# NSA scores: the keys' low parts on 64 rows, with the tiles' query parts in alternate row halves and two tiles beside each other

## What is computed

```
s_s = einsum('bqghd,bgqkld->bghqkl', qb, k_sel) * scale   # selected blocks
s_w = einsum('bqghd,bsgd->bghqs', qb, kw) * scale         # window of 512
o   = gate0 * o_c + gate1 * o_s + gate2 * o_w             # o_s, o_w: softmax(scores - slope*distance) @ values
```

## Time and profile before

| | us |
|---|---|
| median of three executions | 2296.42 |
| the profiled execution, span from its first to its last instruction | 2294.8 |
| the profiled execution's own time | not recorded apart from the span |
| input projection of the NSA mixer, from about | 745 to 832 |
| NSA mix: first scores to last turn, about | 832 to 976 |

### The profile page before, as it was taken

The page is one execution under the profiler, slowest core; times in us unless marked ns, Lnnn a source line. Parts: engine busy times, 40 slices in busy tenths (PEclk is TensorE's granted clock), DMA queues, the critical chain, the costliest instruction groups (busy, mean ns, idle before and its releaser), DMA issues.

```text
span 2294.8 us, 34769 instructions
## 1 busy us (share of the span) xinstructions
PE 2247.6 (98%) x14151; PEld 1950.4 (85%) x14151; DVE 1641.8 (72%) x2121; ACT 1051.0 (46%) x1515; POOL 634.8 (28%) x559
## 2 busy tenths in 40 slices
PE   7999999999999999999999999999999999999999
PEld 5888778999887877778999888999887868899987
DVE  6668557889785456637888657989456984788844
ACT  4322534555334457734555346444345363544432
POOL 0110223332122048803332011332011870233200
PEclk9999999999999999999999999999999999999999
DMA  8654156775763210026774526775333202787322
GB/s 333 191 166 140 46 174 165 185 180 122 267 211 102 82 57 1 1 65 168 190 185 119 162 95 173 175 185 120 101 97 98 81 30 76 191 191 173 105 92 83
DMA packets 224373, 308.69 MB, mean 135 GB/s; under 512 B 14345, under 2 KB 165446, under 8 KB 223958
## 3 DMA queue, kind: packets, MB, share of 16 engines
q1 hardware_dynamic: 173268, 223.99, 30.1%
q0 software_dynamic: 50640, 82.29, 17.4%
q10 hardware_dynamic: 306, 0.19, 0.0%
HBM read 302.23 MB, written 4.19 MB: 134 GB/s over the span
## 4 chain that ended last, share of the span: by engine, by line
PE 85%; DVE 9%; POOL 2%; ACT 2%; issue 1%; DMA 1%; ACTq 0%; DVEq 0%
PE ps L733 42%; PE ps L1181 10%; PE ps L1183 10%; PE ps L1182 10%; PE ps L880 4%; DVE w_lo L2320 2%; DVE dsa_mask L3127 1%; PE ps L1307 1%; POOL nsa_p L3498 1%; PE ps L1323 1%; DVE small L3125 1%; PE ps L929 1%; ACT w_hi L1635 1%; DMA m_raw<-in_ada_w 1%; DVE h_lo L2417 1%
## 5 line engine op out<-in xcount | busy, mean ns | idle before, releaser
L2320 DVE TENSOR_TENSOR w_lo<-w_raw,w_hi 128x1024 fp32r<-128x1024 f32 (+1 forms) x466 | 652.5, 1401 | 478.7 <-ACT w_hi L1635 477.0
L1635 ACT ACTIVATE w_hi<-w_raw 128x1024 fp32r<-128x1024 f32 (+1 forms) x472 | 495.7, 1051 | 996.0 <-PE ps L733 577.6
L1181 PE MATMUL ps<-feat_t,w_hi 128*128 128x256 f32 x1152 | 326.5, 283 | 3.1 <-DVE hid L2824 2.3
L1182 PE MATMUL ps<-feat_t,w_hi 128*128 128x256 f32 x1152 | 326.0, 283 | 0.0
L1183 PE MATMUL ps<-feat_t,w_lo 128*128 128x256 f32 x1152 | 326.0, 283 | 0.0
L3351 POOL TENSOR_TENSOR w_raw<-w_raw,w_raw 128x1024 f32<-128x1024 f32 x72 | 177.7, 2468 | 456.8 <-DVE w_lo L2320 456.8
L733 PE MATMUL ps<-h_hi,w_hi 128*128 128x512 f32 (+1 forms) x712 | 279.7, 393 | 3.8 <-DVE w_lo L2320 2.2
L733 PE MATMUL ps<-h_lo,w_hi 128*128 128x512 f32 (+1 forms) x712 | 277.2, 389 | 0.0
L733 PE MATMUL ps<-h_hi,w_lo 128*128 128x512 f32 (+1 forms) x712 | 277.2, 389 | 0.0
L1181 PE MATMUL ps<-h_hi,w_hi 128*128 128x256 f32 x864 | 244.9, 283 | 1.9 <-DVE w_lo L2320 1.9
L1182 PE MATMUL ps<-h_lo,w_hi 128*128 128x256 f32 x864 | 244.5, 283 | 0.0
(11 more groups left out here) (464 smaller groups left out, 4219.2 us busy)
## 6 DMA issues: line engine op xcount, KB each, us to landing
w_raw<-in_ffn_w_up SPq DMA_DIRECT2D x126, 512.0 KB, 6.5
w_raw<-in_ffn_w_down SPq DMA_DIRECT2D x176, 256.0 KB, 3.3
w_raw<-in_ffn_w_up POOLq DMA_DIRECT2D x72, 512.0 KB, 7.6
m_raw<-in_ada_w POOLq DMA_DIRECT2D x56, 512.0 KB, 4.7
w_raw<-in_ffn_w_gate SPq DMA_DIRECT2D x54, 512.0 KB, 5.9
w_raw<-in_hg_w_in SPq DMA_DIRECT2D x64, 256.0 KB, 3.1
w_raw<-in_ffn_w_up SPq DMA_DIRECT2D x48, 256.0 KB, 3.1
w_raw<-in_nsa_w_in SPq DMA_DIRECT2D x40, 256.0 KB, 2.9
```

What stands on the lines that cost most here:

```text
L1181: K.nc.tensor.matmul(out, hi[:, w], m_hi, start=opens and kt == f == 0, stop=False, skip_group_check=True)
L1182: K.nc.tensor.matmul(out, hi[:, w], m_lo, start=False, stop=False, skip_group_check=True)
L1635: K.nc.scalar.activation(K.half(K.hi(u), width), K.half(K.raw(u), width), ACT.Copy) \
L2320: K.nc.vector.tensor_tensor(K.half(K.lo(u), width), K.half(K.raw(u), width), hi, ALU.subtract) \
```

## The change

The keys' low part is multiplied with the queries' high part alone, on 64 rows; low times low is left out. For tiles 0 and 2 the high part now lies in the other row half and the low part in the head's own half, for tiles 1 and 3 as before. So the two low products of a pair of tiles lie in different row halves. The pairs are (3, 2) and (0, 1); in each, both products over 128 rows come first and then both over 64 rows. In the projection each head's high part and low part are written by two instructions of 64 x 256 instead of one of 64 x 512.

```diff
+def high_rows(head, t):
+    return own_rows(head + (t in (0, 2)))
+
+def token_groups(t):
+    by_tile = t.rearrange("p (a s b) -> p a s b", s=2, b=P)
+    return by_tile[:, :, 0, :], by_tile[:, :, 1, :]
...
-            nc.tensor.matmul(out, K.nq[:, head, tok], K.nk[:, i + 4 * br, 0:w], start=True, stop=False)
-            nc.tensor.matmul(out, K.nq[:, head, tok], K.nk_lo[:, i + 4 * br, 0:w], start=False, stop=True) \
+        def key_high(t):
+            if u:
+                pe.wait_ge(*K["nsa_max"].at((u - 1, SLOTS[SLOT_OF[t]][-1])))
+            w, tok, out = place(t)
+            nc.tensor.matmul(out, K.nq[:, head, tok], K.nk[:, i + 4 * br, 0:w], start=True, stop=False)
+
+        def key_low(t):
+            w, tok, out = place(t)
+            rows = high_rows(head, t)
+            nc.tensor.matmul(out, K.nq[rows, head, tok], K.nk_lo[rows, i + 4 * br, 0:w], start=False, stop=True) \
+                .then_inc(*K["nsa_scores"].up((u, t)))
+
+        for pair in ((3, 2), (0, 1)):
+            for t in pair:
+                key_high(t)
+            for t in pair:
+                key_low(t)
...
-                nc.scalar.activation(K.nq[own, head, :], K.ps[own, b, :], ACT.Copy, scale=0.125).then_inc(*K["query_high"].up(("nsa", head)))
+                for rows, part in ((own, 1), (own_rows(half + 1), 0)):
+                    ins = nc.scalar.activation(token_groups(K.nq[rows, head, :])[part], token_groups(K.ps[own, b, :])[part], ACT.Copy, scale=0.125)
+                ins.then_inc(*K["query_high"].up(("nsa", head)))
...
-                ins = nc.vector.scalar_tensor_tensor(K.nq[other, head, :], K.ps[own, b, :], 0.125, K.nq[own, head, :].bitcast(F32),
-                                                     ALU.mult, ALU.subtract)
+                for high, low, part in ((own, other, 1), (other, own, 0)):
+                    ins = nc.vector.scalar_tensor_tensor(token_groups(K.nq[low, head, :])[part], token_groups(K.ps[own, b, :])[part], 0.125,
+                                                         token_groups(K.nq[high, head, :].bitcast(F32))[part], ALU.mult, ALU.subtract)
```

More of the change, by code:

```diff
@@ L1287, in tensor_nsa_mix, with scores, place @@
     nc, pe = K.nc, K.pe
-    def scores(u, slot):
+    def scores(u):
         i, head, br = unit_of(u)
[L1291 to L1295, removed]
+        def place(t):
+            w = (t + 1) * P
+            return w, slice(t * P, w), K.ps[:, score_bank(t), IN_SLOT[t]:IN_SLOT[t] + w]
+        def key_high(t):
+            if u:
+                pe.wait_ge(*K["nsa_max"].at((u - 1, SLOTS[SLOT_OF[t]][-1])))
+            w, tok, out = place(t)
             nc.tensor.matmul(out, K.nq[:, head, tok], K.nk[:, i + 4 * br, 0:w], start=True, stop=False)
-            nc.tensor.matmul(out, K.nq[:, head, tok], K.nk_lo[:, i + 4 * br, 0:w], start=False, stop=True) \
+        def key_low(t):
+            w, tok, out = place(t)
+            rows = high_rows(head, t)
+            nc.tensor.matmul(out, K.nq[rows, head, tok], K.nk_lo[rows, i + 4 * br, 0:w], start=False, stop=True) \
                 .then_inc(*K["nsa_scores"].up((u, t)))
+        for pair in ((3, 2), (0, 1)):
[3 more added lines that the diff above has]
+                key_low(t)
     def turn(u, bank):
@@ L1381, in tensor_nsa_mix @@
         if n < UNITS:
-            for slot in range(3):
-                scores(n, slot)
+            scores(n)
         if n % 2 == 0 and 1 <= n < UNITS:
```

## The result

The changed kernel takes 2306.7 us (median of 4 executions, 2306.15 to 2309.0), the kernel before 2296.5 us beside it: a ratio of 1.0042, 95% interval 1.003 to 1.0054. It is slower, by 10.2 us where 9.4 were forecast. The profiled execution took 2307.16 us, with a span of 2305.9, which is 11.1 us longer than before; the forecast for the span was 2304.2.

A forecast was written before the change was run, and what follows sets the result against it. TensorE was taken to bound the kernel from 858.69 us on; 10.3 - 1.0 + 0.1 = +9.4 us on the 2294.8 us span gave 2304.2, and 1.6 us more the median, 2305.8 us. Range for 8 in 10: 2302 to 2312.5.

The forecast's parts named there:

- The bound: From 858.69 us to the last unit, a microsecond more of TensorE is one of the kernel, less two GpSimd waits.
- The pairs' gain: Low pairs in each unit: a pair costs its longer member, a gain of 0.28 us a unit.
- A change's price: Each change between 128 and 64 rows: 0.10 us empty array plus 0.11 us open load, 0.2 us together.
- the first rival: Changes of form are free where matmuls follow without a wait: 5.3 us faster, 2291.1 us; chance 7%.
- the fourth: Comes out level: changes partly overlap a stream's end, at half the price, 0.1 us each; about 2296 us; chance 5%.
- the second: Changes cost as said, but pairs of different lengths don't overlap: 7 us more, 2312.8 us; chance 6%.
- The sum for units 6 to 30: 19 units at 0.45 us and 6 at 0.29 us more: 10.3 us, less 1.0 for two GpSimd waits.
- What is late next: Later scores delay VectorE's passes to 3.5 us from unit start; taken at nothing, thin margin at high 2.
- Unit 31 and the tail: Unit 31's tile 3 pass on VectorE starts 0.1 us later, before a tail of latencies: +0.1 us.
- The projection: Split writes in 16 heads: 2.5 us more each on ScalarE and VectorE, hidden beside TensorE; price nothing.
- Units 0 to 5: Ramp units taken at nothing, covered by GpSimd's chain, which was taken to start behind VectorE's work, not TensorE's.
- The third rival: No cover for units 0 to 5 and 31 (+2.9), or TensorE waits for `nsa_max` (+1.2): 2307 to 2310 us; chance 16%.

The follow-up runs named there:

- the run in the same half: Changed kernel's order with the kernel before's layout: 64-row low products, both tiles of a pair in the head's own half; 2315.0 us, ratio 1.0079.
- none in 1.36: Changed kernel with its layout, split writes and order, but low products on all 128 rows again; 2297.6 us, ratio 1.0.
- The run with two changes: Changed kernel, but all four high products of a unit first, then the four low ones, still in pairs; 2302.5 us, ratio 1.0023.
- the kernel with eight changes: Low products in the head's own half, but tile by tile, each high product followed by its low one; 2338.3 us, ratio 1.0177.

## Why the prediction was right, step by step

- **The bound.** TensorE had no room from unit 6 on: its added work, less the two waits that it took up, is the 9.2 us by which these units grew.
- **The pairs' gain**, 0.28 us a unit: the run in the same half gives it back, 7.1 us in 25 units.
- **A change's price**, 0.2 us: four in 1.75 us a unit, eight in 2.72, two in 1.35 and none in 1.36 bear it out. From two to four changes, with the same matmuls on the same rows, a unit grows by 0.40 us. That rules out the first rival (free changes) and the fourth (half the price); the run in the same half rules out the second (no overlap).
- **The sum for units 6 to 30**: 10.3 - 1.0 = 9.3 us, measured 9.2. Units before a turn take 1.75 for 1.35 and their turn 0.06 more, units before values 1.74 for 1.45 (0.29), and both waits for GpSimd are gone.
- **What is late next.** Taken at nothing for TensorE, which was right: it waits for no engine. The working of VectorE's end, 3.5 us after the unit's start, was too late; it is 2.92, and the margin at high 2 is 0.57 us where the working had 0.1. Tile 2's pass starts at 1.82 us, when tile 0's scores are there (906.16 plus the 0.32 us of such a matmul is 1.76 from the start), so nothing was queued behind them. The run with two changes shows how near the wait was: there tile 3's scores come later still, tile 0's pass ends at 2.79, and TensorE waits at 8 units.
- **Unit 31 and the tail**: +0.1, measured 0.1.
- **The projection**: 2.5 us each expected, 2.6 and 2.5 measured, hidden.
- **Units 0 to 5** were taken at nothing, with GpSimd's chain as cover. That step failed, by a small size: the cover starts behind ScalarE's first work, and unit 0's scores stand ahead of the turn of the gates, for which ScalarE waits. Unit 0 costs 0.3 us (the turn of the gates comes 3.60 us after the first scores instead of 3.29), the ramp 0.4 in all.
- **The granted clock** was no term of the sum. In the profiled execution its fall in the ramp added 1.2 us. With the 0.4 above and 0.3 ahead of unit 0, less 0.1 in units 6 to 30, that is, to the rounding, the 1.7 us by which the span exceeded its forecast. The mix (first scores of unit 0 to those of unit 31) came out 10.7 us longer, where the signs named 9 to 10, for the same reason. That the median missed by 0.9 us only is in part luck: it lies 0.8 us above the profiled span, where 1.6 had been taken.
- **The third rival** (no cover or new waits, 2307 to 2310) has its lower edge nearer to the median than the forecast, but not its mechanism: there are no new waits, and missing cover makes 0.4 and 0.1 us of its 2.9.

## What to carry to other kernels

Count changes of the array's form before counting columns. Here one cost 0.2 us, as much as 512 columns of fp32r stream, so a pair of matmuls on half the rows had to save more than that twice over; with 512 beside 384 columns it saved 0.17. Row halves can pay in a long run of such matmuls, like the index scores, which no run here tested. Where a change was due anyway they gave 0.02 us a unit, which no time here can show. When scores are gathered to save changes, ask what comes late: with two changes a unit the wait for the consumer's passes took the place of the changes.

## What the runs showed of the hardware

- Two matmuls in different row halves with 512 and 384 columns, or 128 and 256, take what the longer one takes, and their weight loads are one as well (0.19 us for two). The Trainium skill, page "TensorE: Matmul & The Clock Gate", Part 3, gives the time of a pack as that of one matmul and some 4 ns for each further one; the trace agrees: the second member starts 3 to 4 ns after the first, and the low pair takes 0.42 us where it took 0.60 in the same half.
- A change between 128 and 64 rows cost TensorE some 0.2 us: 0.10 in which nothing streams and 0.11 for a weight load that is no longer hidden (1.65 us for eight in a unit).
- The changed kernel's granted clock fell to 0.50, which is the level of 1.2 GHz, behind a wait of 1.05 us in one execution and stayed at 1.00 behind the same wait in another. Ahead of it stood small matmuls (48 to 128 columns on part of the array) and a unit whose array was empty at four places. A wait isn't needed: the kernel with eight changes fell at the same place behind 0.10 us (its stretch, columns as above):

```profile
840.00:842.00 2.00, 2.00 (x6) 1.58 (x5) 1.97 (x11) 1.73 (x7) 1.51 (x3) 0.50 0.03 8
```

- Where the clock falls differs between executions of one kernel, and a single fall cost 1.2 us in the ramp and 1.5 to 2.3 us near 1780 us, so differences of this size between single executions say little.
